# Column sums over seven tiles, placed ahead of the last tile's products in every LayerNorm

## The reference

```python
mods = (jax.nn.silu(c) @ ada_w[i] + ada_b[i]).reshape(bsz, 9, D_MODEL)
h = _modulate(x, mods, 0)
y = _swiglu(h, ffn_w_in[i, 0], ffn_w_out[i, 0])
x = _layer_norm(ALPHA * x + 0.5 * mods[:, 2, None, :] * y, ln_g[i, 0], ln_b[i, 0], dtype)
h = _modulate(x, mods, 1)
...
def _layer_norm(z, g, b, out_dtype):
    z32 = z.astype(jnp.float32)
    mu = jnp.mean(z32, axis=-1, keepdims=True)
    var = jnp.mean(jnp.square(z32 - mu), axis=-1, keepdims=True)
    return ((z32 - mu) * lax.rsqrt(var + LN_EPS) * g + b).astype(out_dtype)
```

## Time and profile before

| what | us |
|---|---|
| median of 3 runs | 2071.67 (2071.64 to 2075.11) |
| profiled execution | 2071.49 |
| its span, first to last instruction | 2069.8 |
| TensorE matmuls | 2039.3 (99%) |
| TensorE weight loads | 1741.2 (84%) |
| VectorE | 1434.4 (69%) |
| ScalarE | 881.2 (43%) |
| GpSimd | 242.6 (12%) |

### The profile page before, as it was taken

One profiled execution on the slowest core, in us unless ns is written; L12 is line 12 of the kernel. 1 busy time (PEld: TensorE's weight loads), 2 busy tenths in 40 slices (PEclk: granted clock), 3 DMA queues, 4 the chain that ended last, 5 costly groups with the idle time before them and its releaser, 6 DMA issues.

```text
span 2069.8 us, 34112 instructions
## 1 busy us (share of the span) xinstructions
PE 2039.3 (99%) x11850; PEld 1741.2 (84%) x11850; DVE 1434.4 (69%) x2232; ACT 881.2 (43%) x1420; POOL 242.6 (12%) x236
## 2 busy tenths in 40 slices
PE   7999999999999999999999999999999999999999
PEld 6888888878888888888799899878888888988997
DVE  6867767655658767767788378576767568855875
ACT  5222222555535222222545256375656535633642
POOL 0000000432104000001300000142111232000002
PEclk9999999999999999999999999999999999999999
DMA  9767764342324757664333333332222122333332
GB/s 318 245 182 214 219 189 135 97 112 81 91 81 145 226 179 234 205 177 136 92 97 99 109 93 95 114 105 82 71 71 72 50 72 72 109 99 97 103 95 77
DMA packets 405405, 265.96 MB, mean 128 GB/s; under 512 B 9390, under 2 KB 366158, under 8 KB 405332
## 3 DMA queue, kind: packets, MB, share of 16 engines
q1 hardware_dynamic: 405332, 265.06, 43.2%
HBM read 262.86 MB, written 2.19 MB: 128 GB/s over the span
## 4 chain that ended last, share of the span: by engine, by line
PE 93%; DVE 3%; ACT 2%; SPq 1%; POOL 1%; issue 1%; DMA 0%; DVEq 0%; POOLq 0%; ACTq 0%
PE ps L1828 21%; PE ps L1830 21%; PE ps L1829 21%; PE ps L1842 6%; PE ps L1843 6%; PE ps L1844 6%; PE ps L1895 1%; PE ps L1896 1%; PE ps L1920 1%; PE ps L2176 1%; PE ps L2123 1%; PE ps L2108 1%; PE ps L2097 1%; PE ps L2194 1%; PE ps L1901 1%; PE ps L1912 1%
## 5 line engine op out<-in xcount | busy, mean ns | idle before, releaser
L809 ACT ACTIVATE w_hi_all<-raw_all 128x1024 fp32r<-128x1024 f32 (+2 forms) x304 | 286.9, 945 | 741.6 <-PE ps L1830 697.1
L1159 DVE TENSOR_TENSOR w_lo_all<-raw_all,w_hi_all 128x1024 fp32r<-128x1024 f32 (+2 forms) x304 | 333.6, 1100 | 356.7 <-ACT w_hi_all L809 356.2
L1828 PE MATMUL ps<-h_hi,w_hi_all 128*128 128x512 f32 x1104 | 434.6, 394 | 5.0 <-ACT q_sig L892 2.7
L1830 PE MATMUL ps<-h_hi,w_lo_all 128*128 128x512 f32 x1104 | 430.1, 390 | 0.0
L1829 PE MATMUL ps<-h_lo,w_hi_all 128*128 128x512 f32 x1104 | 429.7, 389 | 0.0
L1828 PE MATMUL ps<-g_hi,w_hi_all 128*128 128x512 f32 x704 | 275.0, 391 | 0.0
L1830 PE MATMUL ps<-g_hi,w_lo_all 128*128 128x512 f32 x704 | 274.0, 389 | 0.0
L1829 PE MATMUL ps<-g_lo,w_hi_all 128*128 128x512 f32 x704 | 273.9, 389 | 0.0
L1828 PEld LDWEIGHTS ps<-h_hi,w_hi_all 128*128 128x128 f32 x1104 | 207.2, 188 | 51.7 <-DVE g L1168 3.2
L1830 PEld LDWEIGHTS ps<-h_hi,w_lo_all 128*128 128x128 f32 x1104 | 207.2, 188 | 43.7
L1829 PEld LDWEIGHTS ps<-h_lo,w_hi_all 128*128 128x128 f32 x1104 | 207.3, 188 | 42.0
(11 more groups left out here) (318 smaller groups left out, 3452.2 us busy)
## 6 DMA issues: line engine op xcount, KB each, us to landing
raw_all<-in_ffn_w_in_dram SPq DMA_DIRECT2D x176, 512.0 KB, 3.9
ada_all<-in_ada_w_dram SPq DMA_DIRECT2D x128, 512.0 KB, 4.1
raw_all<-in_ffn_w_out_dram SPq DMA_DIRECT2D x64, 384.0 KB, 3.5
raw_all<-in_ffn_w_out_dram SPq DMA_DIRECT2D x64, 320.0 KB, 3.2
raw_all<-in_hgrn_w_in_dram SPq DMA_DIRECT2D x32, 512.0 KB, 3.7
raw_all<-in_na_w_qkv_dram SPq DMA_DIRECT2D x24, 512.0 KB, 3.8
boot<-in_ada_w_dram SPq DMA_DIRECT2D x8, 512.0 KB, 6.9
boot<-in_ada_w_dram SPq DMA_DIRECT2D x16, 256.0 KB, 6.6
```

Of the source, the lines that this page charges most:

```text
L809: nc.scalar.activation(w_hi[s][:, 0:ph.kt, :], raw[s][:, 0:ph.kt, :], ACT.Copy).then_inc(S.w_hi_done, 1)
L1159: nc.vector.tensor_tensor(w_lo[s][:, 0:ph.kt, :], raw[s][:, 0:ph.kt, :], w_hi[s][:, 0:ph.kt, :].bitcast(F32), ALU.subtract).then_inc(S.w_l ...
L1828: nc.tensor.matmul(ps[:, bank, :], w_hi[s][:, k, :], a, start=start and k == 0, stop=False)
L1830: ins = nc.tensor.matmul(ps[:, bank, :], w_lo[s][:, k, :], a, start=False, stop=stop and k == ph.kt - 1)
```

## The change

In LayerNorms one to five, the zsum group (wait for `zsum_done`, where it applies for `mods_taken`, and four sums) stood in `statistics`, behind the last products. It now stands in `sums_of_seven` ahead of the qsum group, for all six. The rest is as it was, and so is the last LayerNorm (its `mods_taken` wait doesn't apply).

```diff
             def sums_of_seven(ph):
-                if ph.ln == NLN - 1:
-                    pe.wait_ge(S.zsum_done, ph.t0 + KT + 1)
-                    token_sums(6, zsum, True)
+                pe.wait_ge(S.zsum_done, ph.t0 + KT + 1)
+                if ph.ada is not None:
+                    pe.wait_ge(S.mods_taken, ph.ada.n + 1)
+                token_sums(6, zsum, True)
                 pe.wait_ge(S.qsum_done, ph.t0 + KT + 1)
                 token_sums(7, qsum, True)
...
             def statistics(ph):
                 n = ph.ln
-                pe.wait_ge(S.zsum_done, ph.t0 + KT + 1)
-                if ph.ada is not None:
-                    pe.wait_ge(S.mods_taken, ph.ada.n + 1)
-                token_sums(6, zsum, True)
                 last_sums(ph)
```

## The result

The changed kernel takes 2076.47 us (median of 20 executions, 2074.72 to 2080.2); the kernel before 2072.94 us in the same series (20 executions, 2071.06 to 2076.41). The ratio is 1.0016 with a 95% interval of 1.0010 to 1.0022: slower, by 3.3 us (the medians differ by 3.53 us). The forecast was +3.81 us and 2075.5 us.

The account below looks back on a forecast made before the run. TensorE was taken to bound the kernel, its matmuls covering 99% of the span. Lost cover of 3 x 0.84 + 0.63 + 0.66 = 3.81 us on the 2071.67 us median gave 2075.5 us; range 2073.2 to 2077.0 us.

Parts of the forecast that it names:

- The round trip: Last product to VectorE's start 0.43 us, then to loads of x 0.53 us: 0.96 us with nothing standing in it.
- The delay by the moved group: In LayerNorms one to five, the products behind the moved zsum group and VectorE's start come 0.893 us later.
- The two moved waits: TensorE's waits for zsum and the mods at the new place: both ready before TensorE arrives, so neither costs anything.
- VectorE's low parts: Three weight conversions, 3.48 us, make VectorE late after mixers; assumed to stay put, giving prices of 0.63 and 0.66 us.
- lost in full: Rival, chance 0.12: both mixer LayerNorms lose 0.893 us too, 4.31 us in all, 2076.0 us.
- The sum: Five LayerNorms' prices: 3 x 0.84 after feed-forwards + 0.63 + 0.66 after mixers = 3.81 us.
- Swallowed?: Rival, chance 0.13: later TensorE waits absorb the shift, leaving between nothing and some 2 us, 2071.7 to 2073.7 us.
- the clock rival: Chance 0.02: half clock during the sums behind each new gap, 2.68 us more per LayerNorm, 2088.9 us.

## Why the prediction was right

*The round trip.* Its two legs, 0.43 us to VectorE and 0.53 us back, held at all five places within 0.01 us, and their sum of 0.96 us (0.97 at some) is what stands between the last product and x after the change. Both came from rows at places where the leg stood free: the first from feed-forwards, the second from a mixer. That is what let a gap be priced that the trace of before did not have.

*The delay by the moved group.* 0.893 us was forecast; the last product came 0.88 to 0.90 us later than before, counted from the first group. The two moved waits, for zsum and the mods, cost nothing, and VectorE's low parts after the mixers stayed where they were, so the cover was not lost in full there: 0.64 and 0.67 us, not 0.89.

*The sum.* 3.84 us in the trace against 3.81. In the times it is 3.3 us by the ratio (2.1 to 4.6 by its interval) and 3.9 us between the two kernels with the recurrence's wait filled. The traces carry the sum; the times alone would not tell 3.8 us from 3 or 4.5.

*Swallowed?* Between the first and second LayerNorm the shift shrank by 0.31 us (394.82 to 631.82 is 237.00 us, it was 237.31 from 394.07 to 631.38). I first took this for a part of that rival and took the 0.3 us off in the expectations. It is a matter of the execution: in the kernel before with the wait filled, which is the same up to there, the way from the first loads of x to the second LayerNorm's took 239.63 us (394.32 to 633.95) instead of 240.11. The shift itself was not swallowed anywhere that the traces show.

*What was off.* The absolute time: 2076.5 against 2075.5 us. That is in the whole range (2073.2 to 2077.0) but above the one given to the forecast itself (2074.9 to 2076.1), because the three times known beforehand (median 2071.67) held two of the executions without the stretch of low clock, and the median of 20 was 1.3 us higher; from that median the sum would have given 2076.75. That the time still fell into the range owes something to the range's width. And my argument against the clock rival was weak. It said that a wait of 9.60 us at the start left the clock at 1.00; a wait of 2.7 us later on is followed by 1.2 GHz in six of eight profiles. The rival fell on its own ground all the same, since the gaps of this change are under 1 us and none of five is followed by a lower clock. The rule of the Trainium skill (TensorE: Matmul & The Clock Gate, the section on the HAM clock gate), that an idle TensorE goes back to 1.2 GHz, agrees with the trace at the recurrence's start in six of eight profiles; at the kernel's start, behind 9.60 us of idleness, the trace does not show it.

## What to carry to other kernels

Before moving work ahead on a full engine, look at what stands behind it: if the engine's next work needs a round trip through another engine, the work that you move was its cover, and the price at each place is what you move less the slack that it had, by which the data came ahead of the engine (0.05 us here) or another engine was late anyway (0.23 to 0.26 us here). Measure each leg of the round trip where it stands free, and add them. The same order may be right where other work fills the gap, as the last LayerNorm's turned tiles do here (the other order was not tried there), and is wrong in its five siblings; and with effects of a few microseconds look in the traces whether the two profiled executions differ at a place that the change doesn't touch.

## What the runs showed of the hardware

- Behind a wait of TensorE of 2.7 to 2.8 us the granted clock fell to 1.2 GHz in six of eight profiles with this wait open, in the changed kernel's from about a microsecond after work had been taken up again and for some 3 us, at a cost of 1.4 to 1.6 us. With the wait filled by matmuls whose result nobody uses it stayed at 1.00 there in four profiles. Behind the 9.60 us of waiting at the kernel's start it was 1.00.
- In one profile (the filled changed kernel's) it also fell to 0.50 in the last LayerNorm, while TensorE was busy without a gap, with turned tiles and with matmuls whose operands lie on three partitions.
- Column sums with one moving column take as long as with 128 (0.90 and 0.89 us for eight passes at the full clock), and with them the clock fell in five of six LayerNorms of the profile; the kernel took 4 us longer by the medians. The broad, seemingly wasteful form was the faster one.
- VectorE's scaling of p_sb by p_inv (L1272, 128x256) took up to 823 ns in the attention's first step, where GpSimd made the bias beside it, against a median of 349. That GpSimd was the cause was not tried.
